# Modulation slabs beside the attentions: three to five in every second unit instead of one or two in each

## The reference, cut to what matters

```python
m_lat = [m[:, None, :] for m in jnp.split(jax.nn.silu(c) @ ada_w[l] + ada_b[l], 6, axis=-1)]
m_ctx = jnp.split(jax.nn.silu(c_ctx) @ ada_w[l] + ada_b[l], 6, axis=-1)
```

```python
p = jax.nn.softmax(jnp.concatenate([s_loc, s_ctx, sink_q], -1), axis=-1)
a = (p[:, :, 0] - lam * p[:, :, 1]).astype(v.dtype)
```

## Time and profile before

| | |
|---|---|
| time before, median of 3 | 2625.24 us (2623.75 to 2627.37) |
| profiled execution, span from first to last instruction | 2627.1 us (no separate time of this execution is listed) |
| mean granted TensorE clock | 0.989 of full speed |
| PE busy | 2513.8 us, 96% |
| DVE busy | 1625.9 us, 62% |
| ACT busy | 1290.2 us, 49% |
| `block1` attention, about 148.0 to 256.4 us | PE busy 103.27 us, DVE 77.00, ACT 72.46, 234 GB/s |
| `window` attention, about 750.5 to 818.6 us | PE busy 63.48 us, DVE 58.94, ACT 49.59, 248 GB/s |
| `diff_0` attention, about 1407.4 to 1492.7 us | PE busy 81.67 us, DVE 70.62, ACT 63.53, 201 GB/s |

### The profile page before, as it was taken

One profiled execution on the slowest core, in us unless ns is written; L12 is line 12 of the kernel. 1 busy time (PEld: TensorE's weight loads), 2 busy tenths in 40 slices (PEclk: granted clock), 3 DMA queues, 4 the chain that ended last, 5 costly groups with the idle time before them and its releaser, 6 DMA issues.

```text
span 2627.1 us, 42629 instructions
## 1 busy us (share of the span) xinstructions
PE 2513.8 (96%) x16378; PEld 2102.4 (80%) x16378; DVE 1625.9 (62%) x2680; ACT 1290.2 (49%) x2420; POOL 250.8 (10%) x266
## 2 busy tenths in 40 slices
PE   7999999999998999999999999899999999999998
PEld 4855678889857998889886687688889999778887
DVE  2657565553687786668776763433326698775664
ACT  3356454433656764634336733422225644675653
POOL 3000100001202100314000001000002330011000
PEclk8999999999989999999999999999999999999999
DMA  7265522234555455534324535533236454634555
GB/s 281 88 226 184 192 96 96 96 87 136 169 172 190 166 181 171 172 107 153 113 96 145 157 121 180 198 98 97 92 94 175 156 177 163 197 119 137 186 176 150
DMA packets 125611, 393.64 MB, mean 150 GB/s; under 512 B 13776, under 2 KB 24016, under 8 KB 125328
## 3 DMA queue, kind: packets, MB, share of 16 engines
q1 hardware_dynamic: 123584, 386.47, 45.1%
q0 software_dynamic: 1872, 5.02, 0.7%
HBM read 390.39 MB, written 1.05 MB: 149 GB/s over the span
## 4 chain that ended last, share of the span: by engine, by line
PE 82%; DVE 7%; ACT 4%; DMA 3%; issue 2%; POOL 1%; SPq 0%; ACTq 0%; DVEq 0%; POOLq 0%
PE bank L635 21%; PE bank L637 21%; PE bank L636 21%; PE bank L632 4%; PE bank L683 3%; PE bank L818 2%; DVE w_low L1816 2%; PE bank L828 2%; PE bank L631 2%; PE bank L843 1%; ACT w_high L1128 1%; DVE smax L2083 1%; PE bank L841 1%; DMA ring<-in_w_down 1%; PE bank L778 1%
## 5 line engine op out<-in xcount | busy, mean ns | idle before, releaser
L1816 DVE TENSOR_TENSOR w_low<-ring,w_high 128x1024 fp32r<-128x1024 f32 (+2 forms) x604 | 689.9, 1143 | 528.6 <-ACT w_high L1128 525.5
L635 PE MATMUL bank<-h_high,w_high 128*128 128x256 f32 (+1 forms) x2832 | 958.6, 339 | 35.3 <-DVE h_low L2013 11.4
L637 PE MATMUL bank<-h_high,w_low 128*128 128x256 f32 (+1 forms) x2832 | 940.8, 332 | 0.0
L636 PE MATMUL bank<-h_low,w_high 128*128 128x256 f32 (+1 forms) x2688 | 892.4, 332 | 0.0
L1128 ACT CAST w_high<-ring 128x1024 fp32r<-128x1024 f32 (+2 forms) x604 | 576.1, 956 | 264.8 <-DMA ring<-in_w_down 150.5
L635 PEld LDWEIGHTS bank<-h_high,w_high 128*128 128x128 f32 x2832 | 540.7, 191 | 97.0 <-issue 24.3
L637 PEld LDWEIGHTS bank<-h_high,w_low 128*128 128x128 f32 x2832 | 540.7, 191 | 51.1
L636 PEld LDWEIGHTS bank<-h_low,w_high 128*128 128x128 f32 x2688 | 512.5, 191 | 49.9 <-issue 1.7
L635 PE MATMUL bank<-f_high,w_high 128*128 128x256 f32 (+1 forms) x616 | 194.6, 316 | 4.6 <-DVE w_low L1816 4.2
L637 PE MATMUL bank<-f_high,w_low 128*128 128x256 f32 (+1 forms) x616 | 193.0, 313 | 0.0
L636 PE MATMUL bank<-f_low,w_high 128*128 128x256 f32 (+1 forms) x528 | 168.0, 318 | 0.0
(11 more groups left out here) (281 smaller groups left out, 3303.4 us busy)
## 6 DMA issues: line engine op xcount, KB each, us to landing
ring<-in_w_up SPq DMA_DIRECT2D x176, 512.0 KB, 3.5
ring<-in_w_mod SPq DMA_DIRECT2D x112, 512.0 KB, 4.1
ring<-in_w_down SPq DMA_DIRECT2D x80, 384.0 KB, 3.1
ring<-in_w_down SPq DMA_DIRECT2D x80, 320.0 KB, 3.0
spare_slabs<-in_w_mod SPq DMA_DIRECT2D x48, 512.0 KB, 8.0
ring<-in_w_gate SPq DMA_DIRECT2D x48, 512.0 KB, 3.5
ring<-in_w_k SPq DMA_DIRECT2D x32, 512.0 KB, 3.5
ring<-in_w_v SPq DMA_DIRECT2D x32, 512.0 KB, 3.5
```

The source lines that it names most:

```text
L635: pe.matmul(out, wh[:, cols], high, start=first, stop=False)
L636: pe.matmul(out, wh[:, cols], low, start=False, stop=False)
L637: ins = pe.matmul(out, wl[:, cols], high, start=False, stop=last)
L1816: v.tensor_tensor(wl[:, cols], raw[:, cols], wh[:, cols].bitcast(F32), ALU.subtract).then_inc(low_ready, 1)
```

## The change

Only `mods_until` is changed. Slabs now stand only beside odd units, and each part of 16 slabs has a stretch of unit pairs of its own. Pairs of units end the parts at 5, 10 and 15 in `block1`, at 4 and 7 in `window`, at 7 and 14 in `diff_0`.

```diff
         def mods_until(units, slabs, u):

-            if slabs == 48:
-                return min(2 * u, 16 + u)
-            return min(slabs, u * slabs // (len(units) - (2 if units[0]["diff"] else 0)))
+            ends = (5, 10, 15) if slabs == 48 else (4, 7) if len(units) == 16 else (7, 14)
+            part, start = 0, 0
+            for end in ends[:slabs // 16]:
+                if u // 2 < end:
+                    return 16 * part + 16 * (u // 2 - start) // (end - start)
+                part, start = part + 1, end
+            return slabs
```

## The result

The changed kernel is slower. In the first comparison its median was 2637.49 us against 2626.19 (ratio 1.0031, 95% interval 1.0016 to 1.0047), in a second one with more executions 2637.87 against 2627.12 (1.0043, 1.0029 to 1.0056). The forecast was 2625 us and no difference.

The account below looks back on a forecast made before the run. TensorE was taken to bound `block1` and `diff_0`, TensorE and VectorE side by side `window`. Terms -4.0 (`block1`), -2.0 (`diff_0`) and +5.9 (`window`) sum to -0.1 us, set on the 2625.24 us median: 2625 us, range 2621 to 2629.

Parts of the forecast that it names:

- Three falls: -0.1 + 5.1: Rival, chance 0.13: TensorE's clock falls in three stalls of `window`, +5.0 us in all, 2630 us.
- the term for the stalls: `window`: slabs beyond the ring of four wait; +2.6 us each in units 9 and 11, +3.8 in unit 13.
- PEclk 1.00 there: Sign in the profile: TensorE's granted clock stays full at the waits of `window`'s units 9, 11 and 13.
- the mild case: `window`: waits of about 2 us leave TensorE's clock alone, as waits of 1.15 and 2.07 us had.
- +5.9: `window`'s whole change in us: -0.7 + 5.2 + 3.8 - 4.7 = +3.6, with +2.3 for slow landings.
- the 2.3 us counted for slow landings in unit 13: `window`, burst of six: last slabs land after 6.8 us against 4.5, +2.3 us.
- the 0.7 us of gain up to unit 9: `window`: the wait for the copied rows goes, which reached VectorE as 0.74 us of idle; -0.7 us.
- The end of 7.0 us: `window`, unit 13's turning to last values: 7.0 us in place of 11.71, since units 14 and 15 are empty; -4.7 us.
- shrinks to 0.28 us: `block1`: three waits of 0.57 us for ScalarE's copy become four of 0.28, -0.6 us.
- The price of 0.42 us for a slab and 0.13 for an interruption: TensorE: each slab costs 0.42 us, having any slabs in a unit 0.13 us more.
- 2.1 us for interruptions: `diff_0`: 16 units emptied of slabs save 0.13 us each on TensorE, -2.1 us.
- just in time: `diff_0`: VectorE's normalisation barely keeps up in one unit in four; 0.13 us of wait in some five places, +0.7 us.

Follow-up runs that it names:

- fill: Changed kernel plus identity transposes on TensorE ahead of each `window` slab that waits for the ring; 2634.46 us, 7.9 above before's (1.0034).
- d_four: Changed kernel with `window` as before and `diff_0`'s slabs four in every fourth unit; one execution, 2636.14 us.
- b_even: Changed kernel with `window` as before and `block1`'s bursts in even units; 2624.87 us against 2627.12 before (0.999).
- w_spill: Changed kernel with `window`'s slabs beyond four per unit moved to the even units behind; 2627.16 us against 2627.12 before (1.0005).

## Why the prediction was wrong

**The failed step: "Three falls: -0.1 + 5.1", kept as a rival at 0.13.** The prediction counted each wait in `window` by its idle time and let TensorE run on at full clock behind it. The waits came as forecast: 4.93 and 4.89 us per burst of five against 4.7. The step that failed is the term for the stalls, with "PEclk 1.00 there": what it left out is worth 4.6 us by `fill`. The rival's price was nearly right, with two falls in place of three; its chance of 0.13 was too small for a stage in which 7 of 11 such waits brought the clock down. I had two waits of about 2 us that went either way and took the mild case as the likely one. The Trainium skill ("TensorE: Matmul & The Clock Gate", "HAM oscillation — how this bites in real kernels") says of a kernel whose short matmul bursts alternate with DMA waits that the clock goes back at every one of them; here it did at 7 of 11.

**`window` without the falls** took 6.0 us more than before (`fill`), and +5.9 was forecast; that is luck. The fifth slabs landed as forecast (issued at 784.83 and 797.59 us, landing after 3.7 and 3.6 us), but the 2.3 us counted for slow landings in unit 13 hardly came: the burst of six took 814.74 - 808.01 = 6.73 us (6.15 in `fill`), against 4.7 + 1.28 + 2.3 = 8.3, and in `fill` it cost 6.15 - 0.98 = 5.17 us more than the two slabs that stood there, not 3.8 + 2.3 = 6.1. Other misses filled the gap: in `fill` the 0.7 us of gain up to unit 9 is missing (45.91 us to its burst, 45.88 before), and the two pairs from unit 9's burst to unit 13's cost 22.21 - 16.36 = 5.85 us more than before, not 5.2, in part because the old pairs took 8.18 us and not 8.36. The end of 7.0 us was 6.70 in `fill`, and 9.10 in the changed kernel, where 814 to 820 us are at half clock. The 11.71 us with which it was compared vary from 9.5 to 12.6 with the landings, so -4.7 rested on one execution.

**`block1`: the wait "shrinks to 0.28 us" did not.** It should have gone from 1.7 to 1.1 us and went to 2.13, 1.0 of the 1.3 us that are missing. I had put all slab time between the scores and the turning to the wait's credit. But the chain to that turning runs over VectorE: in the changed kernel it begins unit 25's first mask at 226.94 us, with no idle ahead, 1.55 us after TensorE began the scores (225.39); at the like place before it was 1.16 us.

```profile
225.39 1.13 PE L822 MATMUL bank<-big 64*128 64x512 f32 x4
...
226.94 0.42 DVE L2085 TENSOR_TENSOR bank<-bank,big 128x256 f32<-128x256 f32 x1
```

An empty unit brings the scores earlier, to a VectorE that is still busy, and part of the cover that the slabs give is used up by that. The price of 0.42 us for a slab and 0.13 for an interruption held (1.41 us for three).

**`diff_0`: the same error.** The 0.65 us wait of the earlier trace rows went, and of the 2.1 us for interruptions nearly nothing stayed. In most of the empty units with 256 keys the turning starts 0.76 us behind the scores in place of 0.63; the first turning waits 0.72 us (0.18 before), and two at the end 0.29 and 0.22. `d_four` shows whose wait it is. VectorE's being "just in time" meant that TensorE's savings there could not be used.

**What adds up and what does not.** The misses in the table are 1.3 us for `block1`, 1.3 for `diff_0` and 3.7 for `window`, the stages sum to +6.2 or +7.2 us in the two profiles, and the medians say +11.3 and +10.75, with lower ends of 4 and 8. Part of the gap comes from comparing single profiles. Means over all profiles with the same slabs in a stage give `window` 84.73 us (three profiles) against 73.98 (five), `block1` 106.65 (ten) against 108.72 (three) and `diff_0` 86.17 (ten) against 86.57 (three): +10.7 - 2.1 - 0.4 = +8.2 us, which lies inside both intervals. By these means the prediction missed `window` by 4.8 us, about the price of the falls, `block1` by 1.9 and `diff_0` by 1.6.

Code that is the same in all kernels also differs: from `block1`'s end to `window`'s start the 14 profiles took from 3.0 us less to 3.6 more than the first profile of before. The seven with PEclk 1.00 from 690 to 698 us took 483.3 to 486.3 us, the seven below it 486.1 to 489.9. The change may shift falls outside `window` as well: where the first unit of `block1` or `diff_0` has no slab, the clock fell there in 6 of 21 cases, at some 1.5 us each (87.40 and 87.42 us for `diff_0` in place of 85.86), and in none of 7 where it has some. That is too few to show it, and the last 3 us stay open.

No version beat the kernel before clearly; `b_even`, at 0.999, was the best, and its gain is 2 us with an interval that nearly touches none.

## What to carry to other kernels

A burst of work that is longer than its ring buys a full transfer latency (here 3.6 us) for the first element beyond the ring (a second one came 1.3 us later), and the idle time can drop TensorE's clock on top: price the clock with each wait of 2 us and more, and when the rows show both outcomes, let the forecast hold both. The same work one unit later (`w_spill`) cost neither. Savings on one engine count only as far as the engine next to it is free; where two run level, filler work on the one is cover for the other, and an empty unit is no gain. A stage length from a single profile, above all one that ends in transfers, needs a second profile before a difference is built on it: here the mean over five profiles moved the loss of `window` from 9.6 to 10.7 us.

## What the runs showed of the hardware

Waits for DMA between 2.3 and 2.9 us took TensorE from 2.4 to 1.2 GHz in 7 of 11 bursts, not in the order of their length (2.45 did, 2.85 did not); with twenty transposes in the wait it stayed at 2.4 GHz in all three bursts of one profile, two of which stand where it had always fallen. A turning of 1.09 us took 1.90 to 1.97 us at the lower clock. A burst of five 512 KB slabs on a ring of four lasted 4.9 us in place of 2.2 without a wait. The end of the same `window` code, which hangs on slab landings, took 9.49 to 12.55 us in five profiles.
